# Triangular inverse of an RWKV recurrence: four levels and the last one on 32x32 blocks instead of 64x64

## The chip, the cores and the metric

One core of one Trainium2 chip runs the whole kernel. The time is device microseconds of that core for one execution; several executions give a median. The profile is of one separate execution, with its own time.

## The reference

Two blocks of a network, batch 1, 1024 tokens of width 1024, all in float32. The first has an adaptive norm, a token mixer (an RWKV recurrence in both directions over 8 heads of 64, beside differential attention) and a convolutional feed-forward; the second a conformer mixer and gated linear attention. Only the recurrence is touched:

```python
def step(S, inp):
    r_t, w_t, k_t, v_t, kk_t, b_t = inp
    sa = jnp.einsum('bhvk,bhk->bhv', S, kk_t)
    S = (S * w_t[:, :, None, :] - sa[..., None] * b_t[:, :, None, :]
         + v_t[..., None] * k_t[:, :, None, :])
    return S, jnp.einsum('bhvk,bhk->bhv', S, r_t)
```

It runs over 256 context tokens and then 1024 tokens, once forwards and once backwards, for each head.

## The kernel before

Each engine's program is a list of stages: opening, attention (heads, softmax), projections, the recurrence (`scan_...`), its output, mixing, feed-forward, conformer, gated linear attention. A wrapper class issues the instructions, so the profile shows the wrapper's lines: 66 for every `matmul`, 75 for `activation`, 84 for `tt`, 94 for `stt`, 108 for `predicated` (copy where a mask is set).

**The recurrence.** The 1280 positions are cut into 20 chunks of 64. A pair of heads lies in the two halves of the 128 partitions (`HALVES`), so each product of a chunk is two 64x64 matmuls, one per half, on two diagonal tiles of TensorE's array. Four pairs of heads and two directions give eight streams (`STREAMS`), and each has five groups of four chunks: 40 groups (`GROUPS`), 160 chunks. Groups take turns in four sets of tiles (`K.lanes`, `LANES = 4`), and up to four are under way.

Inside a chunk the updates act on one another through a triangular 64x64 matrix, and `(I + L)^-1` of it is wanted. It is built by doubling. `products` (TensorE, line 1422) makes the chunk's matrices, `mask` (VectorE) writes them to A, `first` (line 1679) takes the inverse of blocks of 2 into E, and `first_turn` with `first_out` its transpose into D. Each of `SCAN_LEVELS = range(1, 6)` (line 1132) doubles the block: `level_y` (TensorE, line 1463) multiplies A by D, `turn` (VectorE, line 1687) copies into `K.turn_level` under the mask of the blocks of this level, `level_de` (TensorE, line 1472) makes the new D and E from it, and `de_out` (ScalarE, line 1794) writes both back, from PSUM, 128x512. The fifth level makes only E. For each level all four chunks of the group are done by one step: 8 matmuls for `level_y`, 16 for `level_de` (8 in the last). `solve` uses E. Matrices are 64x64 throughout, although after level 4 the blocks are only 32 wide and everything outside the two diagonal blocks is zero.

Then the chunks follow one another: `take` (TensorE) applies the state, `used` (ScalarE) copies it, `pass` (TensorE) makes the new state, `state` (VectorE) writes it, and the next `take` waits for it. Beside this the factors of the next stream are prepared by VectorE and ScalarE (`sums` to `bonus_terms`), with some wide matmuls (`gates`, `key_norms`, `key_spread`).

**The order.** `scan_steps` (line 1150) lists all steps with engine, price in ns and predecessors. `scan_orders` (line 1237) is a planner that runs when the kernel is built: each step gets a due time, worked back from the last chunk at `PACE` ns a chunk, and each engine takes the step that can start first, and of equals the one that is due first. Four PSUM banks (`K.scan_bank`) go round among the steps that `EVACUATED` names; a step waits until the bank's user of four steps before has been evacuated. Each engine then runs its list strictly in order, with semaphore waits between engines. The planner's prices of the steps of the inverse:

```python
step("t", 500, ("first_turn", gi), ("first", gi))
for li in SCAN_LEVELS:
    last = li == SCAN_LEVELS[-1]
    step("t", 500, ("level_y", gi, li), ("first_out", gi) if li == 1 else ("de_out", gi, li - 1))
    step("v", 440, ("turn", gi, li), ("level_y", gi, li))
    step("t", 500 if last else 930, ("level_de", gi, li), ("turn", gi, li))
    step("s", 390 if last else 610, ("de_out", gi, li), ("level_de", gi, li))
```

TensorE's list has 1,032 steps. The masks are made by GpSimd in the projection stage (`project_pool`, line 1061), the identity tiles of `K.turn_level` at the start of the recurrence (`scan_pool`, line 1826).

Of the kernel before, what the change touches and what calls it, by code (L numbers as in the profile page):

```python
# [1060 lines left out]
def project_pool(K, ge):  # L1061
# [6 lines left out]
    for d, (strict, with_own) in enumerate(((K.before, K.upto), (K.later, K.from_))):  # L1068
        for h, rows in enumerate(HALVES):
# [7 lines left out]
            ge.wait_ge(*G.now())  # L1077
            ge.copy(K.half_level[d][rows], side[rows, 0:6, h * 64:(h + 1) * 64]).then_inc(*G.tick())
    ge.wait_ge(*G.now())
# [51 lines left out]
GROUPS = [(s, n) for s in range(len(STREAMS)) for n in range(5)]  # L1131
SCAN_LEVELS = range(1, 6)

# [5 lines left out]
def group_chunks(gi):  # L1139
# [3 lines left out]

PACE = 5000
HALF = ((0, 640), (640, 1280))
EVACUATED = {"key_norms": "key_roots", "key_spread": "key_scale", "gates": "gate_out", "bonus": "bonus_out", "products": "mask", "first_turn": "first_out",
             "turned": "turned_out", "level_y": "turn", "level_de": "de_out", "solve": "solve_out"}


def scan_steps():  # L1150
# [48 lines left out]
    for gi in groups:  # L1199
# [37 lines left out]
def scan_orders():  # L1237
# [26 lines left out]
    def earliest(at, name):  # L1264
        if name[0] in EVACUATED and len(taken) >= 4:
            user = taken[-4]
            out = (EVACUATED[user[0]], *user[1:])
            if out not in ends:
                return None
            at = max(at, ends[out] + hop["v"])  # L1270
        if name[0] == "turn":
            user = turn_user.get((STREAMS[GROUPS[name[1]][0]][1], name[2]))
            if user is not None:
                if ("level_de", user, name[2]) not in ends:
                    return None
                at = max(at, ends["level_de", user, name[2]] + hop["t"])
        return at

    while len(ends) < len(steps):
        best = None  # L1280
        for e in "tvs":
            choice = None
            for at, name in ready[e]:
                at = earliest(at, name)
                if at is None:
                    continue
                key = (max(at, free[e]), due[name], name[1:])
                if choice is None or key < choice[0]:
                    choice = (key, name)
            if choice is not None and (best is None or choice[0][0] < best[0]):  # L1290
                best = (choice[0][0], e, choice[1])
        start, e, name = best
        ready[e] = [x for x in ready[e] if x[1] != name]
# [4 lines left out]
        if name[0] == "turn":  # L1298
            turn_user[STREAMS[GROUPS[name[1]][0]][1], name[2]] = name[1]
        for x in followers[name]:  # L1300
# [7 lines left out]
def scan_memory(K):  # L1308
# [11 lines left out]
    K.gains = [sb.take(3 * NC) for _ in range(2)]  # L1320
    K.turn_level = [[sb.take(4 * C, u=4) for _ in SCAN_LEVELS] for _ in range(2)]

    def lane_memory(*takes):
        a, t, de = (take() for take in takes)
        return {"A": a.rearrange("p (u x) -> p u x", u=4), "T": t.rearrange("p (u x) -> p u x", u=4), "DE": de,
                "D": de[:, 0:256].rearrange("p (u x) -> p u x", u=4), "E": de[:, 256:512].rearrange("p (u x) -> p u x", u=4)}

# [20 lines left out]

def by_unit(x):
    return x.rearrange("p (u t) -> p u t", t=C)  # L1350

# [28 lines left out]
def scan_tensor(K, te):  # L1380
# [8 lines left out]
    for kind, *at in K.order["t"]:  # L1389
# [45 lines left out]
        elif kind == "first_turn":  # L1435
# [4 lines left out]
            for u in range(4):  # L1440
                for rows in HALVES:
                    done = te.matmul(bank[rows, u * C:(u + 1) * C], g["E"][rows, u, :], K.half_ident[rows, :])
            done.then_inc(*T.tick("first_turn", gi))
# [19 lines left out]
        elif kind == "level_y":  # L1463
# [4 lines left out]
            for u in range(4):  # L1468
                for rows in HALVES:
                    done = te.matmul(bank[rows, u * C:(u + 1) * C], g["A"][rows, u, 0:64], g["D"][rows, u, :])  # L1470
            done.then_inc(*T.tick("level_y", gi, li))
        elif kind == "level_de":
# [4 lines left out]
            bank = open_scan("level_de", gi, li)  # L1477
            if li < SCAN_LEVELS[-1]:
                for u in range(4):
                    for rows in HALVES:  # L1480
                        te.matmul(bank[rows, u * C:(u + 1) * C], g["E"][rows, u, :], turn[rows, u, :])
            for u in range(4):
                for rows in HALVES:
                    done = te.matmul(bank[rows, 256 + u * C:256 + (u + 1) * C], turn[rows, u, :], g["E"][rows, u, :])
            done.then_inc(*T.tick("level_de", gi, li))
        elif kind == "solve":
            gi, = at
            g = K.lanes[gi % LANES]
            te.wait_ge(*latest(S.by("de_out", gi, SCAN_LEVELS[-1]), S.by("turned_out", gi, 0), S.by("turned_out", gi, 1)))
            bank = open_scan("solve", gi)  # L1490
# [49 lines left out]
def scan_vector(K, ve):  # L1540
# [4 lines left out]
    chunked = lambda x: x.rearrange("p (n t) -> p n t", t=C)  # L1545
    turns, last_turn = K.turn_level, {}
    c3, lw3, t13, aa3, kk3 = (chunked(x) for x in (cc, lw, t1, aa, K.kk))
# [7 lines left out]
    for kind, *at in K.order["v"]:  # L1555
# [123 lines left out]
        elif kind == "first":  # L1679
            gi, = at  # L1680
            g = K.lanes[gi % LANES]
            level = K.half_level[1 - STREAMS[GROUPS[gi][0]][1]][:, 0, :]
            ve.wait_ge(*latest(V.by("mask", gi, 0), V.by("mask", gi, 1)))
# [3 lines left out]
        elif kind == "turn":  # L1687
            gi, li = at
            d = STREAMS[GROUPS[gi][0]][1]
            ve.wait_ge(*T.by("level_y", gi, li))  # L1690
            if (d, li) in last_turn:
                ve.wait_ge(*T.by("level_de", last_turn[d, li], li))
            else:
                ve.wait_ge(*G.by("turn_levels"))
            last_turn[d, li] = gi
            ve.predicated(turns[d][li - 1], K.half_level[d][:, li, :].bitcast(I32).unsqueeze(1).broadcast_to([P, 4, C]),
                          by_unit(K.scan_bank.view("level_y", gi, li)[:, 0:256])).then_inc(*V.tick("turn", gi, li))
            K.scan_bank.end(("level_y", gi, li), V.now())
        elif kind == "state":
            gi, ci = at  # L1700
# [20 lines left out]
def scan_scalar(K, se):  # L1721
# [10 lines left out]
    for kind, *at in K.order["s"]:  # L1732
# [48 lines left out]
        elif kind == "first_out":  # L1781
            gi, = at
            se.wait_ge(*T.by("first_turn", gi))
            se.activation(K.lanes[gi % LANES]["DE"][:, 0:256], K.scan_bank.view("first_turn", gi)[:, 0:256],
                          ACT.Copy).then_inc(*S.tick("first_out", gi))
# [8 lines left out]
        elif kind == "de_out":  # L1794
            gi, li = at
            a = 0 if li < SCAN_LEVELS[-1] else 256
            se.wait_ge(*T.by("level_de", gi, li))
            se.activation(K.lanes[gi % LANES]["DE"][:, a:512], K.scan_bank.view("level_de", gi, li)[:, a:512],
                          ACT.Copy).then_inc(*S.tick("de_out", gi, li))
# [26 lines left out]
def scan_pool(K, ge):  # L1826
    scan_start(K, ge)
    for side in K.turn_level:
        for turn in side:
            ge.copy(turn, K.half_ident.unsqueeze(1).broadcast_to([P, 4, C])).then_inc(*K.scan.g.tick("turn_levels"))  # L1830

# [1666 lines left out]
```

## Time and profile before

| | |
|---|---|
| median of 3 runs (lowest, highest) | 3736.47 us (3733.08, 3736.66) |
| the profiled execution: time, span | 3741.04 us, 3739.3 us |
| TensorE busy, share of the span | 3506.3 us, 94% |
| VectorE, ScalarE | 1892.1 us (51%), 945.0 us (25%) |
| the chain that ended last | PE 85%, DVE 9%, ACT 4%, DMA 2% |
| mean granted TensorE clock | 0.970 |

PE is TensorE's matmuls, PEld its weight loads (beside them), DVE VectorE, ACT ScalarE, POOL GpSimd. A float32 product shows as two matmul and two weight-load records. `64*64 64x128` is a tile of 64 rows and 64 columns of the array with a moving operand of 64 partitions by 128 columns. Matmul records overlap, and their ends are modelled: the time of one is a latency, and what a stream of them costs is their busy time over their number.

### The profile page before, as it was taken

Reading aid. Unit: us, or ns where it says so; the run is one execution under the profiler, and the core shown is the slowest. Engines: PE = TensorE matmul, PEld = TensorE weight load, DVE = VectorE, ACT = ScalarE, POOL = GpSimd, SP = SyncE. Lnnn points to the kernel's source line nnn. Section 1 sums busy time; section 2 is a strip of 40 time slices with the busy share of each in tenths; the row PEclk is TensorE's granted clock in tenths of the full one; section 3 lists DMA queues with packets and bytes.
Section 4 is the critical chain, followed back from the end, with each engine's and each line's share of the span. In section 5 each row is a group of like instructions: output and inputs, shape, how many; then the busy total and the mean of one; then the engine's idle time right before and its main releaser. Section 6 shows DMA issues by size and latency. Waiting matters only on the chain.

```text
span 3739.3 us, 63595 instructions
## 1 busy us (share of the span) xinstructions
PE 3506.3 (94%) x28813; PEld 2205.1 (59%) x28813; DVE 1892.1 (51%) x2750; ACT 945.0 (25%) x1867; POOL 49.4 (1%) x114
## 2 busy tenths in 40 slices
PE   7998879989999999789999999998899698999988
PEld 2445655549989899444444444445566345777753
DVE  2037746435555554645555540115999653444524
ACT  3006640125455555220000000100111302233310
POOL 2000000000000000100000000000000000000000
PEclk9999999989999999899999999999999899999999
DMA  6001003200000000321111121113111012010021
GB/s 229 0 14 54 1 23 135 81 6 18 4 18 4 4 4 4 110 94 64 67 57 45 43 93 40 57 51 96 34 34 56 11 63 58 23 34 23 1 84 62
DMA packets 110626, 177.54 MB, mean 47 GB/s; under 512 B 5379, under 2 KB 66562, under 8 KB 109714
## 3 DMA queue, kind: packets, MB, share of 16 engines
q1 hardware_dynamic: 101218, 141.59, 11.3%
q10 hardware_dynamic: 9136, 31.87, 2.4%
q8 instruction: 226, 3.70, 0.4%
q14 instruction: 46, 0.38, 0.0%
HBM read 147.23 MB, written 26.21 MB: 46 GB/s over the span
## 4 chain that ended last, share of the span: by engine, by line
PE 85%; DVE 9%; ACT 4%; DMA 2%; issue 1%; ACTq 0%; SPq 0%; DVEq 0%
PE psum_all L66 83%; ACT sbuf_all L75 3%; DVE sbuf_all L94 3%; DVE sbuf_all L84 2%; DVE sbuf_all L102 2%; PE psum_all L69 1%; ACT L75 1%; DMA sbuf_all<-in_w_mod 1%; DVE sbuf_all L91 0%; DMA sbuf_all<-in_gla_w_out 0%; DVE sbuf_all L108 0%; DMA sbuf_all<-in_w_up 0%; DVE sbuf_all L97 0%; DMA yd_spill<-sbuf_all 0%; DMA sbuf_all<-in_conv_w_in 0%
## 5 line engine op out<-in xcount | busy, mean ns | idle before, releaser
L66 PE MATMUL psum_all<-sbuf_all 64*64 64x64 f32 (+12 forms) x28042 | 3406.6, 306 | 183.4 <-ACT sbuf_all L75 57.6
L66 PEld LDWEIGHTS psum_all<-sbuf_all 64*64 64x64 f32 (+5 forms) x28042 | 2120.3, 153 | 1446.2 <-issue 1032.3
L75 ACT ACTIVATE sbuf_all<-psum_all 128x512 f32<-128x512 f32 (+5 forms) x925 | 409.4, 462 | 1543.4 <-PE psum_all L66 1428.9
L94 DVE SCALAR_TENSOR_TENSOR sbuf_all<-sbuf_all 128x1040 f32<-128x1040 f32 (+8 forms) x571 | 623.5, 1094 | 25.1 <-PE psum_all L66 4.9
L84 DVE TENSOR_TENSOR sbuf_all<-sbuf_all 128x512 f32<-128x512 f32 (+10 forms) x593 | 470.3, 817 | 165.1 <-ACT sbuf_all L75 121.3
L75 ACT ACTIVATE sbuf_all<-sbuf_all 128x64 f32<-128x64 f32 (+10 forms) x454 | 260.9, 584 | 856.4 <-DVE sbuf_all L78 355.2
L78 DVE COPY sbuf_all<-psum_all 128x256 f32<-128x256 f32 (+5 forms) x137 | 71.0, 526 | 472.7 <-PE psum_all L66 459.3
L75 ACT ACTIVATE sbuf_all<-psum_all,sbuf_all 128x1280 f32<-128x1280 f32 (+5 forms) x212 | 163.9, 781 | 342.4 <-PE psum_all L66 326.1
L84 DVE TENSOR_TENSOR sbuf_all<-sbuf_all,psum_all 128x512 f32<-128x512 f32 (+3 forms) x160 | 102.0, 640 | 274.4 <-PE psum_all L66 273.3
L108 DVE COPY_PREDICATED sbuf_all<-sbuf_all,psum_all 128x256 f32<-128x256 int32 (+2 forms) x296 | 145.6, 493 | 159.5 <-PE psum_all L66 154.8
L69 PE MATMUL psum_all<-sbuf_all 128*128 128x128 f32 (+2 forms) x771 | 109.5, 281 | 38.5 <-DVE sbuf_all L84 9.5
L90 DVE TENSOR_SCALAR sbuf_all<-sbuf_all 128x128 f32<-128x128 f32 (+11 forms) x150 | 58.2, 424 | 167.4 <-ACT sbuf_all L75 164.3
L94 DVE SCALAR_TENSOR_TENSOR sbuf_all<-psum_all,sbuf_all 128x64 f32<-128x64 f32 (+4 forms) x192 | 64.9, 353 | 144.2 <-PE psum_all L66 96.9
L75 ACT ACT_TABLE_LOAD x94 | 120.6, 1283 | 43.9 <-PE psum_all L66 31.1
L69 PEld LDWEIGHTS psum_all<-sbuf_all 128*128 128x128 f32 (+2 forms) x771 | 85.9, 144 | 76.0 <-ACT sbuf_all L75 14.5
L84 DVE TENSOR_TENSOR sbuf_all<-psum_all,sbuf_all 128x512 f32<-128x512 f32 (+1 forms) x120 | 73.7, 620 | 81.9 <-PE psum_all L66 79.4
L91 DVE TENSOR_SCALAR sbuf_all<-sbuf_all 128x1024 f32<-128x1024 f32 (+9 forms) x135 | 77.3, 577 | 64.8 <-ACT sbuf_all L75 59.0
L102 DVE TENSOR_REDUCE sbuf_all<-psum_all 128x1 f32<-128x1280 f32 x64 | 95.5, 1492 | 15.3 <-PE psum_all L66 11.3
L94 DVE SCALAR_TENSOR_TENSOR sbuf_all<-sbuf_all,psum_all 128x256 f32<-128x256 f32 (+1 forms) x44 | 24.5, 558 | 105.3 <-PE psum_all L66 104.3
L97 DVE RECIPROCAL sbuf_all<-sbuf_all 128x1 f32<-128x1 f32 (+7 forms) x97 | 23.5, 243 | 91.4 <-ACT sbuf_all L75 91.3
L105 DVE TENSOR_TENSOR_SCAN sbuf_all<-sbuf_all 128x256 f32<-128x256 f32 (+1 forms) x76 | 36.8, 546 | 35.7 <-ACT sbuf_all L75 35.5
L81 POOL MEMSET sbuf_all<- 128x1 f32 (+7 forms) x25 | 6.7, 312 | 2087.9 <-DMA x_spill<-sbuf_all 855.7
(19 smaller groups left out, 140.6 us busy)
## 6 DMA issues: line engine op xcount, KB each, us to landing
sbuf_all<-in_w_mod SPq DMA_DIRECT2D x12, 2048.0 KB, 8.3
sbuf_all<-in_w_up SPq DMA_DIRECT2D x22, 1024.0 KB, 7.7
sbuf_all<-in_w_in SPq DMA_DIRECT2D x6, 2048.0 KB, 8.9
x_spill<-sbuf_all SPq DMA_DIRECT2D x16, 512.0 KB, 2.9
sbuf_all<-in_conv_w_in SPq DMA_DIRECT2D x16, 512.0 KB, 6.3
sbuf_all<-in_gla_w_in SPq DMA_DIRECT2D x8, 1024.0 KB, 5.3
sbuf_all<-in_w_down SPq DMA_DIRECT2D x4, 1792.0 KB, 7.4
hid_spill<-sbuf_all ACTq DMA_DIRECT2D x9, 512.0 KB, 2.6
```

Of the source, the lines that this page charges most:

```text
L66: return self.e.matmul(out, lhsT, rhs, start=start, stop=stop, skip_group_check=True)
L69: return self.e.transpose(out, in_, ident) if self.e is not None else Unissued()
L75: return self.e.activation(out, in_, func, bias=bias, scale=scale, **kw)
L78: return self.e.tensor_copy(out, in_) if self.e is not None else Unissued()
L84: return self.e.tensor_tensor(out, a, b, op) if self.e is not None else Unissued()
L90: return self.e.tensor_scalar(out, a, s1, None, op0)
L91: return self.e.tensor_scalar(out, a, s1, s2, op0, op1)
L94: return self.e.scalar_tensor_tensor(out, a, s, b, op0, op1) if self.e is not None else Unissued()
L97: return self.e.reciprocal(out, a) if self.e is not None else Unissued()
L102: return self.e.tensor_reduce(out, a, AX.X, op, negate=negate)
L105: return self.e.tensor_tensor_scan(out, a, b, 0.0, ALU.mult, ALU.add) if self.e is not None else Unissued()
L108: return self.e.copy_predicated(out, mask, data) if self.e is not None else Unissued()
```

## The change

- Levels 1 to 4 and `first_turn` keep only the two 32x32 diagonal blocks of each 64x64 matrix. The four quarters of the partitions (`QUARTERS`) hold the four blocks of a pair of heads; a product is four 32x32 matmuls on four diagonal tiles instead of two 64x64. D, the new E32 and `K.turn_level` are 32 columns a chunk, not 64; PSUM and copies are half as wide.
- The fifth level becomes steps of its own. `spread` (VectorE, two predicated copies) puts E32 back into the 64-wide E. `last_y` multiplies the off-diagonal 32x32 block of A by D, with the result in the other quarter; `last_turn` (VectorE) copies it, `last_e` multiplies by E32, and `last_out` (VectorE, predicated) writes that block of E. `solve` now waits for `last_out`.
- New masks from GpSimd; new prices for the steps; `PACE` from 5000 to 3600.
- The planner knows the tile size of each step (`tile_mode`), but `CHANGE = 0`: a change of size costs nothing in its choice. The rule of choice is as before.

```diff
-    K.half_level = [sb.view(at + 512 + 384 * d, 384, m=6) for d in range(2)]
+    K.first_level = [sb.view(at + 512 + 64 * d, 64) for d in range(2)]
+    K.turn_mask = [sb.view(at + 640 + 128 * d, 128, m=4) for d in range(2)]
+    K.side_mask, K.quarter_ident = sb.view(at + 896, 64, b=2), sb.view(at + 960, 32)
...
-SCAN_LEVELS = range(1, 6)
+SCAN_LEVELS = range(1, 5)
+QUARTERS = [(slice(32 * n, 32 * n + 32), 32 * (n % 2)) for n in range(4)]
...
-PACE = 5000
+PACE = 3600
...
+BY_32 = ("first_turn", "level_y", "level_de", "last_y", "last_e")
+OTHER_TILES = ("key_norms", "key_spread", "gates")
+CHANGE = 0
...
+def tile_mode(kind):
+
+    return 32 if kind in BY_32 else 128 if kind in OTHER_TILES else 64
...
-        step("t", 500, ("first_turn", gi), ("first", gi))
-        step("s", 390, ("first_out", gi), ("first_turn", gi))
+        step("t", 280, ("first_turn", gi), ("first", gi))
+        step("s", 300, ("first_out", gi), ("first_turn", gi))
         for li in SCAN_LEVELS:
-            last = li == SCAN_LEVELS[-1]
-            step("t", 500, ("level_y", gi, li), ("first_out", gi) if li == 1 else ("de_out", gi, li - 1))
-            step("v", 440, ("turn", gi, li), ("level_y", gi, li))
-            step("t", 500 if last else 930, ("level_de", gi, li), ("turn", gi, li))
-            step("s", 390 if last else 610, ("de_out", gi, li), ("level_de", gi, li))
-        step("t", 500, ("solve", gi), ("de_out", gi, SCAN_LEVELS[-1]), ("turned_out", gi, 0), ("turned_out", gi, 1))
+            step("t", 280, ("level_y", gi, li), ("first_out", gi) if li == 1 else ("de_out", gi, li - 1))
+            step("v", 330, ("turn", gi, li), ("level_y", gi, li))
+            step("t", 530, ("level_de", gi, li), ("turn", gi, li))
+            step("s", 390, ("de_out", gi, li), ("level_de", gi, li))
+        done = ("de_out", gi, SCAN_LEVELS[-1])
+        step("v", 400, ("spread", gi), done)
+        step("t", 280, ("last_y", gi), done)
+        step("v", 300, ("last_turn", gi), ("last_y", gi))
+        step("t", 280, ("last_e", gi), ("last_turn", gi))
+        step("v", 330, ("last_out", gi), ("last_e", gi), ("spread", gi))
+        step("t", 500, ("solve", gi), ("last_out", gi), ("turned_out", gi, 0), ("turned_out", gi, 1))
...
-                key = (max(at, free[e]), due[name], name[1:])
...
+                    change = e == "t" and tile_mode(name[0]) != mode
+                    choices.append((max(at, free[e] + CHANGE * change), due[name], name[1:], name))
...
+def sides(d):
+
+    return (QUARTERS[0::2], QUARTERS[1::2])[::1 if d == 0 else -1]
...
-                for rows in HALVES:
-                    done = te.matmul(bank[rows, u * C:(u + 1) * C], g["A"][rows, u, 0:64], g["D"][rows, u, :])
+                for rows, b in QUARTERS:
+                    done = te.matmul(bank[rows, u * 32:u * 32 + 32], g["A"][rows, u, b:b + 32], g["D"][rows, u, :])
...
+                for (rows, _), (to, b) in zip(*sides(STREAMS[GROUPS[gi][0]][1])):
+                    done = te.matmul(bank[to, u * 32:u * 32 + 32], g["A"][rows, u, b:b + 32], g["D"][rows, u, :])
...
+                for (to, _), (rows, _) in zip(*sides(d)):
+                    done = te.matmul(bank[to, u * 32:u * 32 + 32], K.last_turn[d][rows, u, :], g["E32"][rows, u, :])
```

## Rows read from the trace of the kernel before

**Rows 1.** Cores: span and mean granted clock.
```profile
core 0: 3739.3 us, clock 0.970
```

**Rows 2.** Stages: busy us of each engine (instructions), granted clock, DMA share, GB/s.
```profile
core 0: us, PE busy (x) PEld busy (x) DVE busy (x) ACT busy (x) POOL busy (x), PEclk, DMA share, GB/s
806.00:838.00 32.00, 21.65 (x182) 17.92 (x184) 19.27 (x34) 10.49 (x16) 4.11 (x10) 0.59 0.06 15
838.00:1509.00 671.00, 648.38 (x18750) 613.15 (x18744) 352.15 (x768) 350.33 (x809) 0.00 (x0) 0.98 0.03 8
```

**Rows 3.** Waits, stretch 838 to 1509: total us, times, longest.
```profile
ACT sbuf_all L75 <- PE psum_all L66: 265.9, 348, 5.4
DVE sbuf_all L108 <- PE psum_all L66: 144.0, 117, 3.9
DVE sbuf_all L94 <- PE psum_all L66: 62.0, 48, 2.7
...
DVE sbuf_all L84 <- PE psum_all L66: 44.7, 62, 2.0
...
PE psum_all L66 <- ACT sbuf_all L75: 17.7, 15, 4.2
...
PE psum_all L66 <- DVE sbuf_all L94: 2.4, 10, 0.3
...
PE psum_all L66 <- DVE sbuf_all L84: 1.7, 7, 0.3
```

**Rows 4.** Timeline of TensorE at the end of the stretch: start, us, group.
```profile
1503.79 1.22 PE L66 MATMUL psum_all<-sbuf_all 64*64 64x64 f32 x28 [0.27 <-DVE sbuf_all L94]
1505.28 1.22 PE L66 MATMUL psum_all<-sbuf_all 64*64 64x64 f32 x28 [0.27 <-DVE sbuf_all L94]
```

**Rows 5.** Groups by shape, stretch 838 to 1509: busy us, mean ns, idle before.
```profile
L66 PEld LDWEIGHTS psum_all<-sbuf_all 64*64 64x64 f32 x18480 | 587.8, 136 | 51.2 <-ACT sbuf_all L75 27.6 <-issue 12.5 <-DVE sbuf_all L94 5.3
L66 PE MATMUL psum_all<-sbuf_all 64*64 64x64 f32 x16758 | 531.2, 220 | 21.8 <-ACT sbuf_all L75 17.7 <-DVE sbuf_all L94 2.4 <-DVE sbuf_all L84 1.0
L75 ACT ACTIVATE sbuf_all<-psum_all 128x512 f32<-128x512 f32 x240 | 143.7, 599 | 165.7 <-PE psum_all L66 165.4
...
L108 DVE COPY_PREDICATED sbuf_all<-sbuf_all,psum_all 128x256 f32<-128x256 int32 x200 | 88.8, 446 | 145.4 <-PE psum_all L66 144.0
...
L84 DVE TENSOR_TENSOR sbuf_all<-psum_all,sbuf_all 128x512 f32<-128x512 f32 x76 | 52.4, 691 | 35.2 <-PE psum_all L66 34.8
L75 ACT ACTIVATE sbuf_all<-psum_all 128x256 f32<-128x256 f32 x136 | 51.9, 384 | 44.3 <-PE psum_all L66 43.2
...
L66 PE MATMUL psum_all<-sbuf_all 64*64 64x1 f32 x512 | 15.8, 192 | 0.0
...
L66 PE MATMUL psum_all<-sbuf_all 128*128 128x2 f32 x60 | 7.2, 252 | 0.0
```

**Rows 6.** Weight loads in flight at 968.74, at 968.79 and at 968.94 us.
```profile
968.62 0.26 PEld L66 LDWEIGHTS psum_all<-sbuf_all 64*64 64x64 f32 x6
...
968.68 0.20 PEld L66 LDWEIGHTS psum_all<-sbuf_all 64*64 64x64 f32 x4
...
968.95 0.19 PEld L66 LDWEIGHTS psum_all<-sbuf_all 128*128 128x128 f32 x1
```

**Rows 7.** Timelines of GpSimd, and of TensorE's loads, ahead of the stretch.
```profile
548.31 0.47 POOL L81 MEMSET sbuf_all<- 128x256 f32 x2
806.49 4.11 POOL L78 COPY sbuf_all<-sbuf_all 128x256 f32<-128x256 f32 x10 [257.71 <-ACT sbuf_all L75]
...
719.12 6.23 PEld L66 LDWEIGHTS psum_all<-sbuf_all 64*64 64x64 f32 x98 [0.76 <-issue]
```

More of the change, by code:

```diff
@@ L1077, in project_pool @@
             ge.wait_ge(*G.now())
-            ge.copy(K.half_level[d][rows], side[rows, 0:6, h * 64:(h + 1) * 64]).then_inc(*G.tick())
+            ge.copy(K.first_level[d][rows], side[rows, 0, h * 64:(h + 1) * 64]).then_inc(*G.tick())
+    ge.wait_ge(*G.now())
+    ge.memset(K.side_mask, 0.0).then_inc(*G.tick())
+    for n in range(4):
+        rows, cols = slice(32 * n, 32 * n + 32), slice(32 * n, 32 * n + 32)
+        for d in range(2):
+            ge.wait_ge(*G.now())
+            ge.copy(K.turn_mask[d][rows], K.level["lower" if d == 0 else "upper"][rows, 1:5, cols]).then_inc(*G.tick())
+        ge.wait_ge(*G.now())
+        ge.copy(K.quarter_ident[rows, :], K.ident[rows, cols]).then_inc(*G.tick())
+        ge.wait_ge(*G.now())
+        ge.memset(K.side_mask[rows, n % 2, :], 1.0).then_inc(*G.tick())
     ge.wait_ge(*G.now())
@@ L1270, in earliest @@
             at = max(at, ends[out] + hop["v"])
-        if name[0] == "turn":
-            user = turn_user.get((STREAMS[GROUPS[name[1]][0]][1], name[2]))
+        if name[0] in TURN_READ:
+            user = turn_user.get((STREAMS[GROUPS[name[1]][0]][1], name[0], *name[2:]))
             if user is not None:
-                if ("level_de", user, name[2]) not in ends:
+                if user not in ends:
                     return None
-                at = max(at, ends["level_de", user, name[2]] + hop["t"])
+                at = max(at, ends[user] + hop["t"])
         return at
+    mode = 64
     while len(ends) < len(steps):
@@ L1440, in scan_tensor @@
             for u in range(4):
-                for rows in HALVES:
-                    done = te.matmul(bank[rows, u * C:(u + 1) * C], g["E"][rows, u, :], K.half_ident[rows, :])
+                for rows, b in QUARTERS:
+                    done = te.matmul(bank[rows, u * 32:u * 32 + 32], g["E"][rows, u, b:b + 32], K.quarter_ident[rows, :])
             done.then_inc(*T.tick("first_turn", gi))
@@ L1477, in scan_tensor @@
             bank = open_scan("level_de", gi, li)
[L1478 to L1481, printed above, removed]
+            old = lambda rows, b, u: g["E"][rows, u, b:b + 32] if li == 1 else g["E32"][rows, u, :]
             for u in range(4):
-                for rows in HALVES:
-                    done = te.matmul(bank[rows, 256 + u * C:256 + (u + 1) * C], turn[rows, u, :], g["E"][rows, u, :])
-            done.then_inc(*T.tick("level_de", gi, li))
+                for rows, b in QUARTERS:
+                    te.matmul(bank[rows, u * 32:u * 32 + 32], old(rows, b, u), turn[rows, u, :])
+            for u in range(4):
+                for rows, b in QUARTERS:
+                    done = te.matmul(bank[rows, 128 + u * 32:160 + u * 32], turn[rows, u, :], old(rows, b, u))
+            done.then_inc(*T.tick("level_de", gi, li))
+        elif kind == "last_y":
+            gi, = at
+            g = K.lanes[gi % LANES]
+            te.wait_ge(*S.by("de_out", gi, SCAN_LEVELS[-1]))
+            bank = open_scan("last_y", gi)
+            for u in range(4):
+                for (rows, _), (to, b) in zip(*sides(STREAMS[GROUPS[gi][0]][1])):
+                    done = te.matmul(bank[to, u * 32:u * 32 + 32], g["A"][rows, u, b:b + 32], g["D"][rows, u, :])
+            done.then_inc(*T.tick("last_y", gi))
+        elif kind == "last_e":
+            gi, = at
+            d = STREAMS[GROUPS[gi][0]][1]
+            g = K.lanes[gi % LANES]
+            te.wait_ge(*V.by("last_turn", gi))
+            bank = open_scan("last_e", gi)
+            for u in range(4):
+                for (to, _), (rows, _) in zip(*sides(d)):
+                    done = te.matmul(bank[to, u * 32:u * 32 + 32], K.last_turn[d][rows, u, :], g["E32"][rows, u, :])
+            done.then_inc(*T.tick("last_e", gi))
         elif kind == "solve":
@@ L1795, in scan_scalar @@
             gi, li = at
-            a = 0 if li < SCAN_LEVELS[-1] else 256
             se.wait_ge(*T.by("level_de", gi, li))
-            se.activation(K.lanes[gi % LANES]["DE"][:, a:512], K.scan_bank.view("level_de", gi, li)[:, a:512],
+            se.activation(K.lanes[gi % LANES]["DE"], K.scan_bank.view("level_de", gi, li)[:, 0:256],
                           ACT.Copy).then_inc(*S.tick("de_out", gi, li))
```

82 lines of the change are left out of this document (56 added, 26 removed).

## The prediction

> **What bounds the kernel now.** First the span and the clock of the one core [rows 1]: 3739.3 us at a mean granted clock of 0.970. All the edits lie in the recurrence, so the second view is the table of stages [rows 2]. The recurrence proper (from the first products to the last chunk) is the stretch 838 to 1509 us, 671 us. In it TensorE shows 648 us busy, VectorE 352 and ScalarE 350; SyncE and GpSimd do next to nothing. A busy TensorE may still be idling inside a modelled latency, so the third view is the waits of that stretch [rows 3]: ScalarE and VectorE wait for TensorE for 266, 144, 62 and 45 us, while TensorE waits for them for 17.7, 2.4 and 1.7 us. The stretch is bound by the rate at which TensorE gets through small matmuls. The one serial chain beside it, take, used, pass, state from chunk to chunk, can be read where nothing else is left [rows 4]: the take of a chunk starts 1.49 us after the take before. 160 chunks of that are 238 us, far from 671.
>
> **What a small matmul costs.** Every float32 product is two records (weight load and matmul twice). Grouped by shape [rows 5]: 64x64 tiles with 64 moving columns cost 531.2 us / 16758 = 31.7 ns a record; with one moving column 15.8 / 512 = 30.9 ns. So the moving columns are not what is paid. A full 128x128 tile with 2 moving columns costs 7.2 / 60 = 120 ns. Half the stationary columns, and two tiles of the array side by side instead of one, give a quarter of 120. That is how a weight load of so many columns behaves, with the tiles in parallel. Carried on to 32x32 tiles, four side by side, a record costs 30.9 / 4 = 7.7 ns.
>
> **The sum, part by part.** The reference point is the profiled execution: 3741.04 us, 1.7 us over its span and 4.6 us (0.12%) above the median of the runs, 3736.47.
>
> Blocks of 32. A group of four chunks issued 8 + 40 + 72 = 120 products in first_turn, level_y and level_de, 240 records; 40 groups make 9600. After, first_turn and four level_y have 16 each, four level_de 32 each, last_y and last_e 16 each: 240 products, 19,200 records. By the rows before: 9600 x 30.9 = 297 us. After, by the scaled price: 19,200 x 7.7 = 148 us, a gain of 149. The planner's own prices in the diff give less: per group 0.50 + 5 x 0.50 + 4 x 0.93 + 0.50 = 7.22 us becomes 0.28 + 4 x 0.28 + 4 x 0.53 + 2 x 0.28 = 4.08, 40 x 3.14 = 126. They hold the start of each step, which does not shrink with the tiles, so I take **130 us**, between the two and nearer the second.
>
> Changes of tile size. The order of before has 1,032 steps on TensorE; 87 neighbours differ in tile size. Sorting the same order by the new rule (first_turn and the levels to 32, the rest as it is) gives 667. The number of 32-wide steps per group stays 11 (1 + 4 + 4 + 2 for 1 + 5 + 5), and with CHANGE = 0 nothing keeps equal sizes together, so I take 580 more changes. The price can be read at one that waits for nothing [rows 6]: the last 64-wide loads are over at 968.88 (968.68 + 0.20), so the last of them began at 968.74 (a load takes 0.136, rows 5); the first load of the other size starts at 968.95, 0.21 us later, where two records at 31.7 ns would have brought the next pair after 0.06. That is 0.15 us; the bounds are 0 (TensorE would have stood still anyway) and 0.36 (a matmul of 0.220 and a load of 0.136 one after the other, rows 5). A 32-wide matmul is out sooner, so I take 0.14: 580 x 0.14 = **81 us given back**. The Trainium skill, TensorEngine Tiling (Array Packing), Tiling Modes, says that changing the tiling mode, not just the tile, drains TensorE; it puts no time to it.
>
> VectorE. 200 turns of 446 ns (89 us) become 160 of half the width. The nearest pair of sizes is on ScalarE, 599 ns for 512 columns and 384 for 256; on VectorE 691 for 512 and, another operation, 446 for 256, some 0.96 ns a column, so 128 columns cost about 320. 160 x 320 = 51, spread 2 x 320, last_out 320 and last_turn some 300, 40 times: 50. VectorE gains 12 us of work on 352 in a stretch of some 620: covered by its wait for TensorE [rows 3]. If TensorE were quick enough to need it sooner, the three extra operations (spread is beside last_y, the other two are in line) would add about 0.6 us to a group's latency, which four lanes hide. ScalarE: 40 copies of 384 ns go and 200 get smaller, about 45 us less: nothing on the path. The ring of four banks: 17 of 18 steps a group take one, a step's bank is wanted back four steps later, and evacuations get shorter; nothing. GpSimd makes 17 more small masks at some 0.24 us each in the projection stage: done by 553 instead of 549 us, and TensorE's first user of them comes at 719 [rows 7]. It copies 8 small tiles at 806 instead of 10 (4.11 us, rows 7), long before the first turn: nothing. No DMA is touched.
>
> PACE, and order by urgency: each only reorders. TensorE's real waits are 22 us now [rows 3]; that is all a better order can win and, with TensorE still the busiest by far, about what it keeps. I put nothing.
>
> Sum: 3741.0 - 130 + 81 = 3692, that is 49 below; set against the median, **3687 us**. The stretch would take about 622 us, 3.9 us a chunk.
>
> **The rivals.**
> (a) The forecast, with its own spread: a record at 7.7 to 9, changes at 0.10 to 0.15 us, 550 to 650 of them: from 3645 to 3715. Chance 0.62.
> (b) Slower: a matmul record has a price of its own, whatever its tile. 30.9 ns for one column and 31.7 for 64 would look just the same if it were the cost of issuing a load and a matmul. There are twice as many records, so a fixed price decides. With TensorE bound throughout, gain and loss meet where 19,200 x p = 297 - 81, p = 11 ns. At the full 30.9, 19,200 - 9600 records more cost 297 us: 3736 + 297 + 81 = 4114. At 15 ns it is about 3810. Against it: 120 ns for the 128-wide tile and a quarter of that for two 64-wide ones would be chance. For it: no row shows records following each other in a steady stream faster than 30.9 ns. Chance 0.18 (of it 0.16 over 11.5 ns). The Trainium skill, TensorE: Matmul & The Clock Gate, under "Wait — 56ns, not 53.3ns?", says that starts of matmuls never come closer than about 25 ns however small N is; taken for tiles side by side, 19,200 x 25 = 480 us would be an estimate of about 264 us over now, some 4000 us. This case's row at 30.9 ns does not contradict it.
> (c) The price lies between, 9.5 to 11.5 ns: within noise of 3736. Chance 0.05.
> (d) Changes are cheap, since many fall where TensorE stands still anyway, or cost half: 3736 - 130 + 35 = 3641, or 3619 with 22 us of waits won too. Chance 0.09.
> (e) Changes cost 0.25 and more, or are 900, since shorter steps of more lanes interleave finer; or the drained array lets the granted clock fall. Rows 2 show 0.59 of full speed where TensorE had work for two thirds of the time, 0.98 in the stretch. 900 x 0.15 = 135 gives 3741; 580 x 0.28 = 162 gives 3768; 5% of 622 us at half speed adds 31. Chance 0.06.
>
> **How the numbers follow.** A measurement of this kernel can tell 0.2%, 7.5 us, from no change. Faster: (a) nearly whole, (d): 0.70. Same: (c) and the edges of (a) and (e): 0.08. Slower: (b) over its point and most of (e): 0.22. The range 3635 to 3745 holds (a), (c), most of (d) and the near part of (e): about 0.8. The forecast's own range is 3645 to 3715.
>
> **What the profile after would show.** TensorE's 64x64 records with 64 columns fall from 16,758 to about 7,200 and some 19,000 with 32x32 tiles appear; their busy time over their number is the price: near 8 ns right, 11 and above wrong and (b) true. The stretch shrinks from 671 to about 622 us. At a change of size the loads show a gap like that of rows 6 some 650 times. The first record of a 32-wide step starting 0.15 us after the last 64-wide one confirms the 0.14; 0.3 is (e). ScalarE and VectorE still wait for TensorE for over 300 us. If instead TensorE's waits for the other two pass 60 us, the order or the banks have become the limit and my sum, which has TensorE bound throughout, is the wrong one. The granted clock of the stretch stays at 0.95 or above; everything outside it stays within 3 us.

## The result and the profile after

The changed kernel takes 3886.46 us (median of 4 runs, 3883.87 to 3893.22) against 3736.56 (4 runs, 3733.08 to 3739.55): a ratio of 1.0404 (95% interval 1.0386 to 1.0422), 150 us slower. The profiled execution took 3893.22 us, with a span of 3891.5. Forecast were 3687 us and a range that ended at 3745.

The stretch of the recurrence, by the table of stages of the kernel after, with the columns of [rows 2]. From 838 us it now ends at 1665.53:

```profile
838.00:1665.53 827.53, 704.28 (x26986) 612.72 (x26985) 356.28 (x887) 292.54 (x754) 0.00 (x0) 0.84 0.03 7
```

It grew from 671 to 827.5 us. Work before and behind it is where it was, within 4 us. TensorE has 26,986 records instead of 18,750 [rows 2] and is busy 56 us longer, but 123 us of the stretch lie outside its busy time, where there were 23. The granted clock fell from 0.98 to 0.84. What TensorE waits for, and what the others wait for, in the waits of that stretch (columns of [rows 3]):

```profile
ACT sbuf_all L75 <- PE psum_all L66: 474.5, 407, 5.8
DVE sbuf_all L108 <- PE psum_all L66: 227.8, 131, 5.3
...
PE psum_all L66 <- issue: 112.1, 113, 2.2
...
PE psum_all L66 <- DVE sbuf_all L94: 5.0, 16, 0.5
...
PE psum_all L66 <- ACT sbuf_all L75: 2.4, 7, 0.5
...
PE psum_all L66 <- DVE sbuf_all L84: 1.6, 3, 0.7
```

ScalarE and VectorE wait for TensorE more than before [rows 3]. TensorE waits for them for 9 us. Its idle time is "issue": no semaphore holds it, and yet no instruction starts, 113 times for 112.1 us. In the kernel before the waits of the same stretch have no such row for TensorE's matmuls. The groups by shape of the same stretch (columns of [rows 5]):

```profile
L66 PE MATMUL psum_all<-sbuf_all 64*64 64x64 f32 x7105 | 319.6, 240 | 22.2 <-issue 15.1 <-DVE sbuf_all L94 5.0 <-ACT sbuf_all L75 1.5
L66 PE MATMUL psum_all<-sbuf_all 32*32 32x32 f32 x17888 | 261.2, 206 | 91.6 <-issue 89.8 <-ACT sbuf_all L75 0.8
...
L108 DVE COPY_PREDICATED sbuf_all<-sbuf_all,psum_all 128x128 f32<-128x128 int32 x200 | 60.5, 303 | 230.0 <-PE psum_all L66 227.8
```

The idle time stands ahead of 32-wide records above all. How it comes is to be seen in TensorE's timeline, start, us, group and the idle time before it:

```profile
950.60 2.53 PE L66 MATMUL psum_all<-sbuf_all 32*32 32x32 f32 x128 [1.08 <-issue]
954.33 2.91 PE L66 MATMUL psum_all<-sbuf_all 32*32 32x32 f32 x128 [1.20 <-issue]
958.07 2.19 PE L66 MATMUL psum_all<-sbuf_all 64*64 64x64 f32 x128 [0.83 <-issue]
961.80 2.69 PE L66 MATMUL psum_all<-sbuf_all 32*32 32x32 f32 x128 [1.54 <-issue]
965.53 2.82 PE L66 MATMUL psum_all<-sbuf_all 32*32 32x32 f32 x128 [1.04 <-issue]
```

Each of these groups between two gaps has exactly 128 matmul records, whatever step they belong to. With their weight loads these are 256 instructions. A new group starts every 3.73 us (950.60, 954.33, 958.07, 961.80, 965.53), whether its work takes 2.19 us or 2.91. The page's list of DMA queues has a queue that brings instructions (packets, MB):

```profile
q8 instruction: 291, 4.77, 0.5%
```

4.77 MB in 291 packets are 16 KB each, 64 bytes an instruction if each holds 256. In the stretch of the recurrence it moves 211 packets, and in the same stretch of the kernel before 146:

```profile
q8 instruction: 211, 3.46, 1.8%
```
```profile
q8 instruction: 146, 2.39, 1.5%
```

The records counted in blocks of 128 give 210.8 and 146.5, so this queue brings TensorE's instructions. The times of its packets tie the pauses to it. In the changed kernel 94 matmuls of the stretch start more than 0.5 us after everything before them was over. For eight tenths of them a packet of q8 landed 1.26 to 1.52 us earlier, and the next packet sets out 1.1 us after that start (median). A packet takes 1.0 us. So the queue is not full: 1.4, 1.1 and 1.0 us one after the other are the 3.5 us of a block.

**The theory that the experiments test:** TensorE's instructions arrive in blocks of 256, one block per 3.5 to 3.7 us at best, so a record with its load can't be had for less than 27 to 29 ns however quick the array is. Before, 18,750 records are 146.5 blocks, one in 671 / 146.5 = 4.6 us: the supply ran ahead. After, 26,986 are 211 blocks, at 3.5 us each 738 us for their arrival alone, and where a block's work takes longer than that, the time is not won back in the next one. The Trainium skill, Runtime: NRT & Kernel Launch, Instruction fetch mechanics, says that instructions are refilled in 16 KiB blocks and that the fetch is hidden behind the issue of instructions; the size of a block agrees with the 291 packets, the hiding does not agree with the 112.1 us.

Its rivals: a price of a record on the engine itself, rival (b) of the prediction; the changes of tile size; and the new order and pace of the steps.

### The profile page after: what moved, and what is told of

Read it like the earlier page. It is cut to its first block, busy times and chain, and to the rows that moved or that the text cites. A ratio compares the mean times of both kernels' runs of the same rounds, so it can differ in the third digit from the quotient of the medians.

```text
span 3891.5 us, 80355 instructions
## 1 busy us (share of the span) xinstructions
PE 3558.9 (91%) x37133; PEld 2205.7 (57%) x37133; DVE 1896.5 (49%) x2870; ACT 887.9 (23%) x1815; POOL 50.4 (1%) x129
## 3 DMA queue, kind: packets, MB, share of 16 engines
q8 instruction: 291, 4.77, 0.5%
## 4 chain that ended last, share of the span: by engine, by line
PE 83%; DVE 8%; issue 4%; ACT 3%; DMA 2%; SPq 0%; ACTq 0%; DVEq 0%
PE psum_all L66 82%; DVE sbuf_all L94 3%; ACT sbuf_all L75 3%; DVE sbuf_all L102 2%; DVE sbuf_all L84 2%; PE psum_all L69 1%; DMA sbuf_all<-in_w_mod 1%; DVE sbuf_all L91 0%; ACT L75 0%; DMA sbuf_all<-in_gla_w_out 0%; DVE sbuf_all L108 0%; DMA sbuf_all<-in_w_up 0%; DVE sbuf_all L97 0%; DMA yd_spill<-sbuf_all 0%; DMA sbuf_all<-in_conv_w_in 0%
## 5 line engine op out<-in xcount | busy, mean ns | idle before, releaser
L66 PE MATMUL psum_all<-sbuf_all 32*32 32x32 f32 (+10 forms) x36362 | 3459.7, 285 | 282.7 <-issue 112.1
L66 PEld LDWEIGHTS psum_all<-sbuf_all 32*32 32x32 f32 (+4 forms) x36362 | 2121.1, 144 | 1597.9 <-issue 1160.5
L75 ACT ACTIVATE sbuf_all<-psum_all 128x256 f32<-128x256 f32 (+5 forms) x885 | 363.6, 422 | 1737.7 <-PE psum_all L66 1606.3
L78 DVE COPY sbuf_all<-psum_all 128x256 f32<-128x256 f32 (+7 forms) x177 | 82.4, 472 | 495.5 <-PE psum_all L66 481.9
L108 DVE COPY_PREDICATED sbuf_all<-sbuf_all,psum_all 128x128 f32<-128x128 int32 (+1 forms) x296 | 117.2, 397 | 243.8 <-PE psum_all L66 238.1
```

Source lines behind the costliest of these rows:

```text
L66: return self.e.matmul(out, lhsT, rhs, start=start, stop=stop, skip_group_check=True)
L75: return self.e.activation(out, in_, func, bias=bias, scale=scale, **kw)
L78: return self.e.tensor_copy(out, in_) if self.e is not None else Unissued()
L108: return self.e.copy_predicated(out, mask, data) if self.e is not None else Unissued()
```

## The experiments

Two kernels take instructions away and leave the order of steps as it is after. **shared_e**: one product of 128 columns for each quarter, instead of four of 32, in the E half of every level.

```diff
-            for u in range(4):
-                for rows, b in QUARTERS:
-                    done = te.matmul(bank[rows, 128 + u * 32:160 + u * 32], turn[rows, u, :], old(rows, b, u))
+            new = lambda rows, b: g["E"][rows, :, b:b + 32] if li == 1 else g["E32"][rows, :, :]
+            for rows, b in QUARTERS:
+                done = te.matmul(bank[rows, 128:256], turn[rows, 0, :], new(rows, b))
```

> The changed kernel with one edit: in level_de the product for E takes the first chunk's turn tile as the weights for all four chunks, 4 matmuls of 128 moving columns instead of 16 of 32 (so E32 of chunks 2 to 4 is another quantity than the reference's). Order, changes of tile size, copies and waits stay. It issues 12 x 4 levels x 40 groups = 1920 products, 7680 TensorE instructions, 30 blocks of 256, fewer. Supply theory (TensorE runs out of instructions; a block of 256 cannot come faster than one per 3.5 us): 30 x 3.5 = 105 us less, about 3780. Tile-change theory (what was lost is 595 drained changes): the array's own time falls by 5 us at most and the changes stay, 3880. Fixed price per record of 15 ns: 3840 records less, 58 us less, 3828.

Measured: 3795.74 us (3779.87 to 3801.90), ratio to before 1.0141 (1.0114 to 1.0168). That is 91 us under the changed kernel, for 30 blocks fewer, 3.0 us each: between the 105 us of the supply theory and the 58 us of a fixed price, and far from the tile-change theory. The instruction queue of the page and TensorE's wait:

```profile
q8 instruction: 261, 4.28, 0.5%
```
```profile
PE psum_all L66 <- issue: 64.7, 79, 2.6
```

**shared_all** does the same in level_y and in the D half as well:

```diff
-            for u in range(4):
-                for rows, b in QUARTERS:
-                    done = te.matmul(bank[rows, u * 32:u * 32 + 32], g["A"][rows, u, b:b + 32], g["D"][rows, u, :])
+            for rows, b in QUARTERS:
+                done = te.matmul(bank[rows, 0:128], g["A"][rows, 0, b:b + 32], K.lanes[gi % LANES]["DE"][rows, 0:128])
...
-            for u in range(4):
-                for rows, b in QUARTERS:
-                    te.matmul(bank[rows, u * 32:u * 32 + 32], old(rows, b, u), turn[rows, u, :])
+            for rows, b in QUARTERS:
+                te.matmul(bank[rows, 0:128], old(rows, b, 0), turn[rows, :, :])
```

> As shared_e, with level_y and both products of level_de on shared weights (the inverse of chunks 2 to 4 is another quantity than the reference's): 36 x 4 x 40 = 5760 products, 23,040 instructions, 90 blocks fewer than the changed kernel, under the kernel before in number. All changes of tile size stay. Supply theory: TensorE is bound by the array and the changes again, the gaps at block ends vanish, and my sum of the prediction holds: about 3690 (3660 to 3720), below the kernel before. Tile-change theory: 15 us less than the changed kernel, 3870. Fixed price of 15 ns a record: 11,520 x 15 = 173 us less, 3713.

Measured: 3666.65 us (3642.57 to 3671.28), ratio 0.9795 (0.9762 to 0.9828), 220 us under the changed kernel. Its stage, its wait and its timeline, each of TensorE, and two of its groups by shape:

```profile
838.00:1443.00 605.00, 588.85 (x15495) 480.75 (x15489) 349.85 (x887) 289.85 (x756) 0.00 (x0) 0.94 0.03 8
```
```profile
PE psum_all L66 <- issue: 1.4, 2, 1.1
```
```profile
947.75 30.12 PE L66 MATMUL psum_all<-sbuf_all 32*32 32x128 f32 x492
```
```profile
L66 PE MATMUL psum_all<-sbuf_all 64*64 64x64 f32 x7134 | 286.2, 227 | 8.5 <-DVE sbuf_all L94 6.6 <-ACT sbuf_all L75 1.2
L66 PE MATMUL psum_all<-sbuf_all 32*32 32x128 f32 x3840 | 164.5, 288 | 4.2 <-ACT sbuf_all L75 1.9 <-issue 1.1 <-DVE sbuf_all L84 0.8
```

The stretch is 605 us long, the idle time on issue is 1.4 us, and a run of 30 us has no gap. The steps, their tile sizes and their order are those of the changed kernel; the instructions and where they end are what differs. So neither the changes of size nor the order make up the 150 us. The page's instruction queue has 201 packets, 90 fewer than in the changed kernel.

The two stretches differ by 222 us. 111 of them are idle time on issue (112.1 - 1.4). The rest lies in TensorE's busy time, and it is split here by the distances between the starts of neighbouring records in the two traces. In the changed kernel a 64-wide record of 64 columns takes 31 ns at full clock and 54 at half, a 32-wide one of 32 columns 9.5 and 14.2; in shared_all one of 128 columns takes 24.0 at full clock. Summed over all records, the half clock costs the changed kernel some 97 us and this one 37, 60 us between them. The other part is that four 32-wide records of 32 columns (38 ns) cost the array more than one of 128 columns (24), where the expectations had put 5 us at most: some 48 us. As estimates, 111, 60 and 48 make 219 of the 222. So shared_all is not the changed kernel with the supply taken away; that would stand near 3667 + 48 = 3715 us, still under the kernel before.

**change200** has CHANGE = 200 for 0, so that the planner keeps steps of one size together.

> The changed kernel with CHANGE = 200 in the planner instead of 0: 347 changes of tile size in TensorE's order instead of 595, same instructions. Tile-change theory (they are the loss, some 150 to 230 us): at least 248 x 0.3 = 75 us less, under 3810. Supply theory: as many instructions come at the same rate, and the changes lie inside the time of waiting for them: 0 to 25 us less, 3860 to 3886.

Measured: 3970.00 us (3962.93 to 3972.74), ratio 1.0617 (1.0601 to 1.0633), 84 us above the changed kernel, with 347 changes of size in place of 595. Both theories missed. The stage, the wait and the group of 32-wide records:

```profile
838.00:1743.84 905.84, 710.66 (x27059) 639.08 (x27053) 355.33 (x889) 293.42 (x756) 0.00 (x0) 0.77 0.03 7
```
```profile
PE psum_all L66 <- issue: 163.2, 119, 2.7
```
```profile
L66 PE MATMUL psum_all<-sbuf_all 32*32 32x32 f32 x17920 | 257.0, 212 | 157.9 <-issue 150.7 <-ACT sbuf_all L75 4.7 <-DVE sbuf_all L84 2.0
```

The number of instructions is the same. The stretch is 78 us longer: 51 us are more idle time on issue (163.2 against 112.1), 21 are waits for the other engines (30 against 9), and only 6 are busy time, though the clock fell from 0.84 to 0.77. The pauses grew ahead of the 32-wide records (150.7 us against 89.8). A reading that fits, argued and not shown: a row of 32-wide steps outruns the supply by more, and the 64-wide steps between them, which before took 4.6 us a block, no longer let it catch up. That the changes of size are the loss is refuted; fewer of them made it slower.

**refilled** is shared_all with its instructions given back: behind each product of 128 columns, three rounds of the four quarters with one column.

```diff
+            for _ in range(3):
+                for rows, b in QUARTERS:
+                    te.matmul(bank[rows, 0:1], old(rows, b, 0), turn[rows, 0, 0:1])
```

> shared_all with the number of instructions brought back to that of the changed kernel and next to nothing else: behind each set of 4 wide products, 12 products of one column on 32x32 tiles that write one column again (5760 products, 23,040 instructions, 90 blocks; the inverse of chunks 2 to 4 stays another quantity than the reference's). Supply theory: back to the changed kernel's time, 3860 to 3920. Array alone (7.7 ns a record for 11,520 records): 89 us over shared_all's 3667, about 3755.

Measured: 3951.57 us (3941.18 to 3962.31), ratio 1.0571 (1.0542 to 1.0601). The one-column products bring shared_all from 3667 to 3952, by 285 us where the array alone was expected to add 89, and the instruction queue has its 291 packets again. That a price on the engine would do this too is settled by the next experiment; that the result is above the changed kernel's 3886 was not expected. Its stage:

```profile
838.00:1730.36 892.36, 818.81 (x26985) 724.83 (x26982) 358.07 (x887) 292.93 (x754) 0.00 (x0) 0.79 0.03 7
```

TensorE is busy 115 us longer than in the changed kernel, since the wide products cost more on the array than 32 columns do, and the clock is lower, 0.79. It is idle on issue for 63.9 us. So of the 285 us only 62 are pauses. By the distances between starts, as an estimate, the 11,520 added records take some 100 us of the array (8.8 ns each at full clock) and the lower clock about as much again. The run shows that instructions with hardly any work in them are dear here; it does not separate the supply from the clock. And it has the lower clock of the two with about half of the pauses, so pauses alone do not set the clock.

**bursts** takes the kernel before and puts, after everything of the recurrence is done, three bursts of independent products on TensorE: 512 with 64-wide tiles, 1536 with 32-wide ones and 256 with 32-wide ones and 256 columns. Nothing in them waits.

```diff
+    te.wait_ge(*V.final())
+    te.wait_ge(*S.final())
+    for tiles, wide, cols, calls in ((HALVES, 64, 64, 512), ([rows for rows, _ in QUARTERS], 32, 32, 1536),
+                                     ([rows for rows, _ in QUARTERS], 32, 256, 256)):
+        for i in range(calls // len(tiles)):
+            for rows in tiles:
+                te.matmul(K.used_bank_all[rows, 0:cols], K.ident[rows, 0:wide], K.ident_wide[rows, 0:cols])
```

> The kernel before with three bursts of matmuls of the identity, needed by nobody, at the end of the recurrence on TensorE alone: 512 products on 64x64 tiles with 64 columns, then 1536 on 32x32 tiles with 32 columns, then 256 on 32x32 tiles with 256 columns. Supply theory, 3.5 us for 256 instructions: the middle burst is 6144 instructions, 24 blocks, 84 us with a gap about every 256 instructions; the first 8 blocks, 29 to 30 us, no gaps; the last 4 blocks, 27 us, no gaps (array-bound, 53 ns a record). Sum about 142 us more than before. If only the array counts (7.7 ns a record), the middle burst takes 24 us, sum 81. A fixed price of 15 ns a record gives 46 us for it, evenly spread.

Measured: 4366.13 us in one execution. It can't be compared: the chip granted it a lower clock from the recurrence on (0.823 over the span, against 0.970 of the kernel before). Its 32-wide burst still has groups of 128 records, 3.5 to 4.0 us apart. So the same kernel ran again:

> The same kernel as bursts, whose one execution ran under a lower granted clock from the recurrence on. At the full clock: the middle burst of 24 blocks at 3.48 to 3.6 us each, 84 to 86 us, the granted clock at 0.5 in it; all three bursts 142 to 150 us, and the whole 3880 to 3900.

Measured: 3887.27 us in one execution, 147.7 over the 3739.55 of the kernel before beside it. TensorE's timeline and the stages of the three bursts:

```profile
1519.24 24.95 PE L66 MATMUL psum_all<-sbuf_all 64*64 64x64 f32 x896 [2.27 <-issue]
1546.27 1.27 PE L66 MATMUL psum_all<-sbuf_all 32*32 32x32 f32 x128 [2.08 <-issue]
1550.29 1.93 PE L66 MATMUL psum_all<-sbuf_all 32*32 32x32 f32 x128 [2.75 <-issue]
1553.77 1.93 PE L66 MATMUL psum_all<-sbuf_all 32*32 32x32 f32 x128 [1.56 <-issue]
1557.26 1.93 PE L66 MATMUL psum_all<-sbuf_all 32*32 32x32 f32 x128 [1.56 <-issue]
...
1624.45 1.92 PE L66 MATMUL psum_all<-sbuf_all 32*32 32x32 f32 x128 [1.82 <-issue]
```
```profile
1519.00:1544.00 25.00, 24.76 (x896) 24.69 (x896) 0.00 (x0) 0.00 (x0) 0.00 (x0) 0.93 0.02 5
1550.00:1625.00 75.00, 39.10 (x2601) 36.49 (x2604) 0.00 (x0) 0.00 (x0) 0.00 (x0) 0.50 0.02 4
1630.00:1666.00 36.00, 36.00 (x526) 30.29 (x518) 0.00 (x0) 4.20 (x7) 0.00 (x0) 0.96 0.01 2
```

The view of the DMA queues from 1550 to 1625 us has 20 packets of instructions:

```profile
q8 instruction: 20, 0.33, 1.7%
```

This is the supply by itself. From 1550.29 to 1624.45 a block of 128 records comes every 3.71 us on average (20 blocks in 74.16 us), 29 ns a record. The whole burst took some 87 us where 84 to 86 were expected. The array had the 128 records of 1546.27 done in 1.27 us, with 8.5 ns between their starts. Later it took 1.93, at the clock of 0.50 to which it fell with half of each period idle. So the engine has no price of 15 or 30 ns per record; within a block records follow each other at 8.5. The first row of the timeline merges two kinds: its 896 records are seven blocks, 749 of the 64-wide burst (31.2 ns a record, 4.0 us a block) and the first 147 of the 32-wide one, without a gap between. So 64-wide work is slower than the supply and has no gap inside those blocks, nor has the burst with 256 columns.

**shared_all_change200** asks what a change of size costs where the supply does not bind: shared_all with CHANGE = 200.

> shared_all in the order of change200: 347 changes of tile size instead of 595, few enough instructions that supply should not bind. My price of a change, 0.137 us: 248 x 0.137 = 34 us under shared_all, 3633. If a change costs 0.3 us: 75 under, 3592. If the grouped order itself is worse, whatever the supply (TensorE waits for VectorE and ScalarE instead): at or above 3667.

Measured: 3667.51 us (3660.27 to 3669.05), ratio 0.9812 (0.9796 to 0.9829), the same as shared_all. The stage and the waits of TensorE:

```profile
838.00:1430.33 592.33, 556.75 (x15469) 477.44 (x15464) 344.79 (x886) 287.90 (x754) 0.00 (x0) 0.95 0.03 8
```
```profile
PE psum_all L66 <- DVE sbuf_all L84: 13.3, 4, 3.8
PE psum_all L66 <- DVE sbuf_all L94: 9.9, 20, 1.2
PE psum_all L66 <- ACT sbuf_all L75: 8.9, 14, 1.4
```

The stretch is 13 us shorter and holds 32 us of waits for the other engines where shared_all had 13. So 248 changes less save (13 + 19) / 248 = 0.13 us each, as an estimate: the stages are those of the slowest execution of shared_all and the fastest of this kernel, and by the medians it would be 0.07. In the changed kernel's trace two records on either side of a change start 0.149 us apart at full clock (424 pairs), which fits 0.13. The order that saves them gives most back as waits.

**last_alone** is the kernel before with the last level alone on 32-wide blocks (233 changes of size, 1280 records of 32-wide tiles, no more instructions in all than before).

```diff
-SCAN_LEVELS = range(1, 6)
+SCAN_LEVELS = range(1, 5)
...
+            for u in range(4):
+                for (rows, own), (to, b) in zip(*sides(STREAMS[GROUPS[gi][0]][1])):
+                    done = te.matmul(bank[to, u * 32:u * 32 + 32], g["A"][rows, u, b:b + 32], g["D"][rows, u, own:own + 32])
```

> The kernel before with the last level alone on compact blocks (last_y, last_turn, last_e, last_out, with the 64-wide D and E; no spread), levels 1 to 4 as before, PACE 5000. The two steps issue 8 products each, as before: no instruction is added. Array: 2 x (464 - 248) ns a group, 17 us less; changes of tile size 233 instead of 87, 146 x 0.137 = 20 us more. Supply theory: no gap at block ends, nothing lost there: 3732 to 3755. If 32x32 tiles or drained changes were the loss in themselves: 40 groups of 11 such steps cost 150 us, so two of eleven should cost 27 us or more, over 3765.

Measured: 3734.59 us (3733.65 to 3738.42), ratio 0.9999 (0.9989 to 1.0008): no change that can be told, as the supply theory had it. Its group of 32-wide records:

```profile
L66 PE MATMUL psum_all<-sbuf_all 32*32 32x32 f32 x1280 | 34.9, 193 | 0.1
```

Their starts lie 16.5 ns apart, not 8.5: these two steps work on two 32-wide tiles side by side, not on four. So 1280 x (29.6 - 16.5) = 17 us are saved and (233 - 87) x 0.13 = 19 given back, which leaves nothing. Where the number of instructions stays, nothing is lost.

**before_pace3600** and **after_pace5000** exchange the planner's PACE.

```diff
-PACE = 5000
+PACE = 3600
```

> The kernel before with PACE = 3600 instead of 5000 and nothing else. If PACE only reorders, as I predicted: within 8 us of before, 3730 to 3746. If it is part of the loss: over 3760.

Measured: 3735.58 us, ratio 0.9991 (0.9982 to 1.0000): nothing that can be told.

> The changed kernel with PACE = 5000 again: 590 changes of tile size for 595, same instructions. Supply theory: 3870 to 3905. If the new pace is part of the loss: under 3860.

Measured: 3935.03 us (3933.01 to 3939.42), ratio 1.0536 (1.0519 to 1.0554), 49 us above the changed kernel and above every expectation. The wait of its stretch:

```profile
PE psum_all L66 <- issue: 124.0, 113, 4.2
```

As in change200, an order alone moves the time by tens of us once the supply binds, and not before. Which steps stand together in a block may decide it; no run shows it.

No version that beats the kernel before and computes the whole was found. shared_all, 70 us under it, leaves out the separate blocks of three chunks in four. Mixing 64-wide and 32-wide levels within the 3.5 us per block was not tried.

## Why the prediction was wrong

**What bounds it**: right for the kernel before, but only half seen. TensorE's records were the limit, and the limit was read as the array's alone. The row that spoke of the supply was [rows 2] itself: 18,750 records in 671 us are 36 ns a record, 4.6 us per 256 instructions, where the chip can bring them in 3.7: 24% of headroom. A change that takes 44% more records had to ask what the engine is fed with.

**Price of a record**: close for the array. 7.7 ns was forecast; the first 32-wide block of the burst ran at 8.5, and the changed kernel's records start 9.5 ns apart at full clock, which on 16,640 records is 30 us more. The test that the prediction named, busy time over number, gives 261.2 / 17,888 = 14.6 ns, and 11 and above was to mean (b). It would have named the wrong cause: it takes in the half clock (14.2 ns a record) and the ends of the steps.

**Count**: last_y and last_e have 8 products each, not 16. That makes 448 records a group, 17,920 in all and not 19,200 (the trace has 17,888). At 7.7 ns that is 10 us too much. But on two tiles instead of four such a record costs 16.5 ns (last_alone): 1280 x 16.5 = 21 us, where 2560 x 7.7 = 20 were taken. Two errors cancelled, by luck.

**Changes of size**: 595 against 87 before, 508 more where 580 were taken, at 0.13 us where 0.14 was taken: 66 us instead of 81. With the changes as measured the sum would have been 3741 - 130 + 66 = 3677, or 3672 set against the median. That shared_all came out at 3667 does not confirm it, since it also spares the array some 48 us; with the estimate of 3715 for the changed kernel without the limit of the supply, the forecast was some 40 us too low even there, by the price of a record and by the clock.

**VectorE, ScalarE, GpSimd**: right. The turns take 303 ns where 320 was forecast, and their waits for TensorE grew. **PACE**: "I put nothing" holds on the kernel before (0.9991) and fails on the changed one, where it is worth 49 us.

**The step that failed** is the sum itself, "TensorE bound throughout" at 9600 x 30.9 against 19,200 x 7.7. It took the busy array for the engine's rate and gave the arrival of instructions no term. In its place the runs show 211 blocks that can't come faster than one in 3.5 us, 112 us of gaps, and some 85 us more from the lower clock (97 against 12 in the kernel before, an estimate from the distances of starts). The prediction's sign for the clock, 0.95 or above in the stretch, failed with 0.84. The test named in the prediction, TensorE's waits for the other two passing 60 us, did not meet it: those waits fell to 9 us, and the idle time was on issue.

**Rival (b)** had the direction and the reason, twice the instructions. It had the mechanism wrong: a price per record on the engine, no wait for delivery. At the supply's 28 ns it would have given some 4060 us, for it counted the price for the 32-wide records alone and not as a bound over all, where slow 64-wide steps (31.7 ns) leave supply to spare. The Trainium skill, TensorE: Matmul & The Clock Gate, under "Wait — 56ns, not 53.3ns?", gives 25 ns as the closest distance of two starts; across four tiles side by side the burst contradicts it, with 128 records in 1.27 us. **Rival (e)** named a drained array that lets the clock fall and put 31 us to it: the fall was there, to 0.84, but not through the changes of size: they were as many in shared_all, where the clock kept 0.94. It comes with more and smaller instructions; how much of it the pauses make is not shown, since refilled has 0.79 with 63.9 us of them.

## What to carry to other kernels

Before making tiles smaller, count instructions per microsecond in the stretch: a stream of loads and matmuls at under about 28 ns a pair is bound by the arrival of its instructions, and shows it as idle time on "issue" in front of groups of 128 records or multiples of it, each start some 1.4 us behind the landing of an instruction packet. Products that share a weight load or take more columns per instruction are what gains there; more and smaller ones don't. Look at the granted clock as well: it was 0.77 to 0.90 in the kernels here that had such a stream, and in the changed kernel it cost some 85 us beside the 112 us of gaps. The two do not go one to one: change200 has 51 us more of gaps and 6 us more of busy time.

## What the runs showed of the hardware

Instructions come in blocks of 256, 3.71 us apart when nothing else limits them, and hardly ahead: the burst of 32-wide tiles has its first gap at the first block boundary that it meets (1546.27), 147 records in, behind 64-wide work that took 4.0 us a block. A packet takes 1.0 us, the block starts 1.4 us behind its landing, and the next packet sets out 1.1 us behind that. Why the queue does not run further ahead stays open. The granted clock follows: 0.93 in the 64-wide burst, 0.50 in the 32-wide one with its engine half idle, 0.96 in the one with 256 columns. Half clock costs small records less than large ones: 13.3 ns for 8.5 on 32-wide tiles in the burst, 54 for 31 on 64-wide ones in the changed kernel. And four 32-wide tiles side by side really run in parallel, at 8.5 ns a record, two of them at 16.5.
